# A two-block network on one core: the condition spread by transposes, small operations and row copies moved behind the second unit's split, and that unit's first half split in two pieces

## The reference, cut to what matters

```python
L, D = 272, 1024
xn = rms_norm(h, norm_g)                                   # first layer's head
q, k, v, f_logit, o_gate = split(xn @ w_in)                # (272,1024) @ (1024,4112)
...
mod = (silu(c) @ w_ada + b_ada).reshape(b, 3, 3, D)        # second block
u = rms_norm_2(h, norm_pre[i]) * (1.0 + scale) + shift
h = h + resid_w * gate * rms_norm_2(fn(u), norm_post[i])
```

## Time and profile before

| what | value |
|---|---|
| time, median of 3 runs | 1295.34 us (1295.28 to 1295.97) |
| the profiled execution's own time | 1294.34 us |
| its span, first to last instruction | 1291.9 us |
| PE busy | 1283.2 us (99%) |
| DVE busy | 941.0 us (73%) |
| ACT busy | 626.4 us (48%) |
| POOL busy | 63.0 us (5%) |
| mean granted TensorE clock | 0.999 |

### The profile page before, as it was taken

One profiled execution on the slowest core, in us unless ns is written; L12 is line 12 of the kernel. 1 busy time (PEld: TensorE's weight loads), 2 busy tenths in 40 slices (PEclk: granted clock), 3 DMA queues, 4 the chain that ended last, 5 costly groups with the idle time before them and its releaser, 6 DMA issues.

```text
span 1291.9 us, 27214 instructions
## 1 busy us (share of the span) xinstructions
PE 1283.2 (99%) x11138; PEld 1243.7 (96%) x11138; DVE 941.0 (73%) x1200; ACT 626.4 (48%) x745; POOL 63.0 (5%) x102
## 2 busy tenths in 40 slices
PE   9999999999999999999999999999999999999998
PEld 9988899999999999999999999999999899999986
DVE  7666788998567866888875877667977667966644
ACT  6356554434354345543443643443555674743433
POOL 3000000000002000000000000000011000000000
PEclk9999999999999999999999999999999999999999
DMA  8542256666646333565666467766485335466553
GB/s 289 201 134 82 105 203 207 215 225 231 244 158 217 134 127 124 208 219 201 210 246 229 164 239 271 262 236 231 165 276 208 128 134 186 164 219 240 191 170 124
DMA packets 40408, 252.36 MB, mean 195 GB/s; under 512 B 4544, under 2 KB 4800, under 8 KB 16144
## 3 DMA queue, kind: packets, MB, share of 16 engines
q1 hardware_dynamic: 29232, 211.89, 47.2%
q0 software_dynamic: 10816, 39.32, 8.9%
q10 hardware_dynamic: 288, 0.13, 0.0%
HBM read 250.27 MB, written 1.05 MB: 195 GB/s over the span
## 4 chain that ended last, share of the span: by engine, by line
PE 95%; DVE 2%; ACT 2%; issue 1%; DVEq 0%; ACTq 0%
PE ps L2319 78%; PE ps L3035 5%; PE ps L2357 2%; PE ps L2575 1%; PE ps L2452 1%; DVE w_lo L1173 1%; ACT w_hi L497 1%; PE ps L2705 1%; ACT scratch L732 1%; PE ps L2754 1%; PE ps L2808 1%; PE ps L2423 1%; PE ps L3008 0%; PE ps L2535 0%; PE ps L2586 0%
## 5 line engine op out<-in xcount | busy, mean ns | idle before, releaser
L497 ACT ACTIVATE w_hi<-raw 128x2048 fp32r<-128x2048 f32 (+1 forms) x178 | 352.4, 1980 | 407.2 <-PE ps L2319 346.4
L1173 DVE TENSOR_TENSOR w_lo<-raw,w_hi 128x2048 fp32r<-128x2048 f32 (+1 forms) x177 | 420.2, 2374 | 140.1 <-ACT w_hi L497 138.3
L2319 PE MATMUL ps<-x_hi,w_hi 128*128 128x272 f32 (+2 forms) x1504 | 432.3, 287 | 0.1
L2319 PE MATMUL ps<-x_hi,w_lo 128*128 128x272 f32 (+2 forms) x1504 | 426.8, 284 | 0.0
L2319 PE MATMUL ps<-x_lo,w_hi 128*128 128x272 f32 (+2 forms) x1344 | 382.8, 285 | 0.0
L2319 PEld LDWEIGHTS ps<-x_hi,w_hi 128*128 128x128 f32 x1504 | 283.3, 188 | 5.4 <-issue 3.7
L2319 PEld LDWEIGHTS ps<-x_hi,w_lo 128*128 128x128 f32 x1504 | 283.6, 189 | 0.0
L2319 PEld LDWEIGHTS ps<-x_lo,w_hi 128*128 128x128 f32 x1344 | 253.0, 188 | 0.1
L2319 PE MATMUL ps<-proj_r,w_hi 128*128 128x256 f32 (+2 forms) x1312 | 234.1, 281 | 0.3 <-issue 0.2
L2319 PEld LDWEIGHTS ps<-proj_r,w_hi 128*128 128x128 f32 x1312 | 201.5, 188 | 1.0 <-issue 0.7
L2319 PE MATMUL ps<-proj_r,w_lo 128*128 128x256 f32 (+2 forms) x656 | 184.3, 281 | 0.0
(11 more groups left out here) (408 smaller groups left out, 1610.2 us busy)
## 6 DMA issues: line engine op xcount, KB each, us to landing
raw<-in_units_ffn_up SPq DMA_DIRECT2D x44, 1024.0 KB, 5.0
raw<-in_units_glu_up SPq DMA_DIRECT2D x44, 1024.0 KB, 5.0
v_tok<-in_w_ada_t POOLq DMA_DIRECT2D x72, 512.0 KB, 3.7
raw<-in_units_ffn_down SPq DMA_DIRECT2D x16, 1408.0 KB, 5.9
raw<-in_units_mix_in SPq DMA_DIRECT2D x20, 1024.0 KB, 5.2
raw<-in_units_hgrn_in SPq DMA_DIRECT2D x16, 1024.0 KB, 4.9
raw<-in_units_fox_in SPq DMA_DIRECT2D x14, 1024.0 KB, 5.0
raw<-in_units_glu_down SPq DMA_DIRECT2D x8, 1408.0 KB, 5.9
```

The costliest lines, as they stand in the source:

```text
L497: nc.scalar.activation(w_hi[s][:, 0:size], raw[s][:, 0:size], ACT.Copy).then_inc(hi_ready, 1)
L1173: V.tensor_tensor(w_lo[s][:, 0:size], raw[s][:, 0:size], w_hi[s][:, 0:size].bitcast(F32), ALU.subtract).then_inc(lo_ready, 1)
L2319: ins = T_.matmul(dst, fixed, moving, start=(kt == 0 and i == 0), stop=(kt == kts - 1 and i == 2), skip_group_check=first)
```

## The change

On PE, the eight matmuls that spread the condition become transposes of the same broadcast columns. On ACT, the two copies to `c_row` move behind unit 1's split, and the first half of unit 1 is split in two activations of 128x512, with a signal each (`part_hi`, `half_hi`). On DVE, the nine small operations move from ahead of the first `x_lo` to behind unit 1's second half, ahead of `sum_squares`; `w_lo` of unit 1's first half is made in two pieces (`part_lo`, `half_lo`). PE waits for the first piece at tile 0 of unit 1 and for the second at tile 2. A later count of `part_hi` is one higher. The functions `first_tiles_lo` and `first_weights_lo` are moved as they are.

```diff
@@ ScalarE
             for g in range(4):
                 first_tiles_hi(g)
                 first_weights_hi(g)
+            act.wait_ge(w_half_landed, 16)
+            for quarter, done in ((slice(0, UNIT // 4), part_hi), (slice(UNIT // 4, UNIT // 2), half_hi)):
+                nc.scalar.activation(w_hi[1][:, quarter], raw[1][:, quarter], ACT.Copy).then_inc(done, 1)
+            act.wait_ge(raw_landed[1], 16)
+            nc.scalar.activation(w_hi[1][:, UNIT // 2:UNIT], raw[1][:, UNIT // 2:UNIT], ACT.Copy).then_inc(hi_ready, 1)
             for n, bank in enumerate((5, 7)):
                 act.wait_ge(c_spread, n + 1)
                 nc.scalar.activation(c_row[:, n * 512:(n + 1) * 512], ps[:, bank, :], ACT.Copy).then_inc(c_row_set, 1)
-            act.wait_ge(w_half_landed, 16)
-            nc.scalar.activation(w_hi[1][:, 0:UNIT // 2], raw[1][:, 0:UNIT // 2], ACT.Copy).then_inc(half_hi, 1)
-            act.wait_ge(raw_landed[1], 16)
-            nc.scalar.activation(w_hi[1][:, UNIT // 2:UNIT], raw[1][:, UNIT // 2:UNIT], ACT.Copy).then_inc(hi_ready, 1)
@@ VectorE, behind c_ready
+            for g in range(4):
+                first_tiles_lo(g)
+                first_weights_lo(g)
+            dve.wait_ge(part_hi, 4)
+            V.tensor_tensor(w_lo[1][:, 0:UNIT // 4], raw[1][:, 0:UNIT // 4], w_hi[1][:, 0:UNIT // 4].bitcast(F32), ALU.subtract).then_inc(part_lo, 1)
+            dve.wait_ge(half_hi, 1)
+            V.tensor_tensor(w_lo[1][:, UNIT // 4:UNIT // 2], raw[1][:, UNIT // 4:UNIT // 2], w_hi[1][:, UNIT // 4:UNIT // 2].bitcast(F32),
+                            ALU.subtract).then_inc(half_lo, 1)
+            second_half_lo("fox_in")
             for i in range(2):
                 V.tensor_scalar(qk_gain[:, i:i + 1], cols[:, 0, Q_GAIN_ROW:Q_GAIN_ROW + 1], Q_SCALE, None, ALU.mult)
...
             V.tensor_tensor(lb_tmp[1], l1, lb, ALU.subtract).then_inc(exp_inputs, 1)
-            for g in range(4):
-                first_tiles_lo(g)
-                first_weights_lo(g)
-            first_half_lo(1)
-            second_half_lo("fox_in")
             sum_squares(0, L)
@@ TensorE
-                    ins = T_.matmul(ps[:, bank, i * P:(i + 1) * P], c_silu[:, k:k + 1].to_broadcast([P, P]), ident, start=True, stop=True)
+                    ins = T_.transpose(ps[:, bank, i * P:(i + 1) * P], c_silu[:, k:k + 1].to_broadcast([P, P]), ident)
@@ first_pair, unit 1
                     if kt == 0:
+                        pe.wait_ge(part_lo, 4)
+                    if kt == KD // 4:
                         pe.wait_ge(half_lo, 1)
                     if kt == KD // 2:
                         pe.wait_ge(lo_ready, 4)
```

More of the change, by code:

```diff
@@ L1187, in split_lo_half @@
                 else:
-                    dve.wait_ge(part_hi, 3 + n + 1)
+                    dve.wait_ge(part_hi, 4 + n + 1)
                 half = slice(part * size // 2, (part + 1) * size // 2)
@@ L1369, in _ @@
             V.tensor_tensor(c_silu, c_silu, vecs("c_2", 0, KD), ALU.mult).then_inc(c_ready, 1)
[L1370 to L1378, removed]
             def first_tiles_lo(g):
@@ L1394, in _ @@
                 first_weights_lo(g)
-            first_half_lo(1)
-            second_half_lo("fox_in")
+            dve.wait_ge(part_hi, 4)
[3 more added lines that the diff above has]
+                            ALU.subtract).then_inc(half_lo, 1)
+            second_half_lo("fox_in")
+            for i in range(2):
+                V.tensor_scalar(qk_gain[:, i:i + 1], cols[:, 0, Q_GAIN_ROW:Q_GAIN_ROW + 1], Q_SCALE, None, ALU.mult)
+                V.tensor_copy(qk_gain[:, 2 + i:3 + i], cols[:, 0, K_GAIN_ROW:K_GAIN_ROW + 1])
+            V.tensor_scalar(subln, vec("da_subln_2"), 1.0 - LAMBDA_INIT, None, ALU.mult)
+            l0, l1 = vecs("hgrn_lower_bounds", 0, KD), vecs("hgrn_lower_bounds", KD, KD)
+            steps.done(V.tensor_tensor(lb, l0, l1, ALU.max))
+            steps.wait()
+            V.tensor_tensor(lb_tmp[0], l0, lb, ALU.subtract)
+            V.tensor_tensor(lb_tmp[1], l1, lb, ALU.subtract).then_inc(exp_inputs, 1)
             sum_squares(0, L)
```

## The result

The kernel with the change takes 1298.47 us (median of 13 runs, 1297.04 to 1302.72); in the same sessions the kernel before takes 1295.34 (13 runs, 1294.38 to 1297.68). The ratio is 1.0023 [1.0016, 1.0030]: 3.1 us slower. Forecast was 1295.65, with a range up to 1296.9; the median lies 1.6 us above that range, so the forecast was wrong. "Same" had been given 0.97, with its line drawn at 0.2%; the interval of the ratio lies on both sides of that line. The profiled execution took 1299.32 us, with a span of 1297.6.

The account below looks back on a forecast made before the run. PE was taken as the bound, busy 1283.2 of 1291.9 us. Front gain 0.5, sum chain 0.63 later, additions 0.3 shorter gave restart +0.3: 1294.34 to 1294.65, plus 1.0 for the median, 1295.65; range 1294.6 to 1296.9.

Parts of the forecast that it names:

- Moved DMAs: none but this. So the 0.3 us goes to the end: Behind the late sum: only SP's unit 3 issue moves, 0.3 us earlier, so PE's 0.3 us loss reaches the end.
- the unseen: Anywhere in the kernel: something the prediction had not thought of; no size given, chance 0.05.
- The spread and the front: Start of the head: transposes save 1.4 us, first product at 6.85, 0.7 us earlier; 0.5 us kept at unit 1.
- rival 2: PE in the head: the step to full clock comes later, first products at half pace; +1.2 us, 1296.5, chance 0.08.
- The gain at unit 1: Head: PE starts unit 1 at 13.05 instead of 13.56 us, 0.5 us won.
- The late sum: Head, after unit 1's products: PE arrives at 17.6, waits 1.0 us for DVE's additions, restarts at 18.61 instead of 18.30.
- the turn with POOL: DVE's additions ahead of the late sum: one instead of two is blocked by POOL's SBUF reads, costing 0.6 us.
- Nothing waits at unit 2: Behind the late sum: w_lo and the first bank are ready by 22.75, before PE needs them at 23.4 us.
- The head's price at the end: End of the kernel: the late sum's 0.3 us delay arrives there as 0.3 us lost.
- Gain kept: Rival on the late sum: additions meet no POOL work or ACT's copies end sooner; restart 18.0, 1295.0 us, chance 0.22.
- Slower clock by the transposes: The same case as rival 2: transposes and idle PE delay the full clock in the head; +1.2 us, chance 0.08.
- No effect: Rival on the head: front gain and late sum cancel within 0.1 us, 1295.35 us; chance 0.15.

Follow-up runs that it names:

- The padded change: The changed kernel with four small unread float32 matmuls behind the spread, putting 16 instructions back into PE's program: 1296.25 us, ratio 1.0002 to the kernel before.
- half-padded kernel: The kernel before with the spread's transposes alone and two small dummy matmuls, 8 PE instructions fewer than before: 1295.06 us, ratio 1.0003.

## Why the prediction was wrong

**The step that failed** is "Moved DMAs: none but this. So the 0.3 us goes to the end", in the part on what lies behind the late sum. I followed every buffer, bank and DMA behind the head, but not PE's own program. The part on the front counted that the transposes make 8 passes where the matmuls make 16, and stopped there. The same count says that 16 instructions go, and that every later instruction of PE stands 16 places earlier against the blocks in which code is fetched. Its price is 2.5 to 2.8 us in the profiles. In medians: 2.7 us for the transposes alone, and none once the 16 are put back. The profile of before gave no price for it; what it showed is the risk, dense small matmuls beside full weight loads, and a queue of code packets of 16 KB. I had given the unseen a chance of 0.05.

**The spread and the front** met their number by luck. First product 6.93 (6.85 foretold). The transposes were to be over by 6.2, 0.11 us apart, and `x_lo` and `w_lo` to bind; they ran 0.21 apart, the last started at 6.89, and the product followed it, with `w_lo` ready since 5.96 + 0.68 = 6.64. The step to the full clock that rival 2 put at 5.3 in the kernel before came at 6.4 there: only the first six of the sixteen passes were slow, which a median of 275 ns does not show. The gain at unit 1 was not kept: in this execution `h`'s second group came late (ACT waited 1.27 us), PE idled 0.96, and unit 1 began at 14.22, not 13.05. In the other executions with the small operations moved, unit 1 began from 13.3 to 14.2 (13.65 before). The landings scatter by more than the gain of 0.5; it is not to be found in any median.

**The late sum** decides, as argued, and PE idles for it; size off. The sum was to end at 18.46 and ended at 19.57. The difference splits so: the second half of unit 1 landed at 12.8 instead of 12.0, and DVE's last `w_lo` of it began at 13.93 instead of 13.15, 0.78 later; the turn with POOL fell on the small operations (0.29 + 0.83 more than their 0.16 each, 1.12), of which 0.25 was covered by the wait for the squares; and the additions, free of it, took 2.71 instead of 3.26, 0.55 less. 18.46 + 0.78 + 1.12 - 0.25 - 0.55 = 19.56. DVE and not ACT's squares bound the first addition, against the forecast. I had written that the cast "meets only small operations" and priced that at nothing, and had `w_f_lo` meet an addition and not a small operation: the cover of 0.25 was too thin. On the split of unit 1's first half in two: PE waited for neither piece, and what it is worth was not tried by itself. Why unit 1's halves land at 10.8 in the kernel before and from 10.6 to 11.6 in the others stays open: kernels with the same head differ by as much.

**Nothing waits at unit 2:** that held. Its first product follows PE's queue at 24.73 without a wait, though `w_lo` came 0.6 later than before (20.28 beside 19.68). The wait of 0.5 us for a `w_lo` in the list above is another unit's, at 537.36.

**The head's price at the end.** The trace has unit 2 start 1.4 us later. The padded change, which has that head and no stall, is at 1.0002 [0.9993, 1.0011]: +0.3 us, between -0.9 and +1.4. Foretold were 0.3. That agrees, but does not test it: the interval also holds zero and 1.4, the restart is 1.1 later than foretold, and the two medians stand 0.8 apart.

**The rivals.** Gain kept: no. Slower clock by the transposes: no, its sign and size came out for another reason. The transposes did run at the slower pace in the changed kernel, but so did the first passes before, and the step comes as early with transposes as without in other executions; the products kept their pace. No effect: true of the head alone, within what can be measured.

## What to carry to other kernels

Count the instructions that an edit takes out of or adds to an engine's program, not only their time: everything behind it shifts against the blocks in which code is fetched, and a stretch of small matmuls beside a full weight load can run dry, here 400 us later. When a small edit moves the end by microseconds and its own neighbourhood doesn't show it, compare the two traces instruction by instruction for where the lead jumps, and put the removed instructions back as idle ones: if the time returns, it was the place of the code and not its work. And a step priced at nothing because 0.25 us of slack covers it deserves its own bound: here an operation of 0.16 us that met a longer one of GpSimd took that one's time.

## What the runs showed of the hardware

- 256 PE instructions last 16 us in products of 128x272 and 1.3 us in score products of 128x32 and smaller. A packet of code that moves during those reaches PE too late: it restarts 2.2 to 2.4 us behind the start of the packet, in eight stalls of four profiles (in the changed kernel the packet moves between 426.3 and 426.8, the restart is at 428.97).
- A shift of 16 instructions costs 2.5 to 2.8 us, one of 8 nothing: here the effect is a threshold, not a slope.
- A DVE operation of 128x8 with two SBUF inputs, 0.16 us alone, took 0.99 us beside a POOL operation of 1.02 us that reads SBUF: to 0.01 us the same in four executions of three kernels. In one where POOL came later, it took 0.16. An operation of 128x1 with one SBUF input, started 0.02 us behind POOL's cast in the same four, kept its 0.14.
- The 128x128 passes of the head go from 0.21 to 0.11 us apart at 5.3 to 7.7 us, scattered, in thirteen profiles with eight warm-up matmuls, whether they are transposes or float32 matmuls; with four warm-ups all sixteen passes and the first products were slow, 0.21 and 0.23 us apart, until 9.6.
- In the half-padded kernel PE idled for 2.6 us up to 983.4, and the granted clock read 0.50 for 3.4 us, from 985.2 to 988.6; the products start 0.22 us apart there instead of 0.12.
